# A mixture of experts whose rows go back to their tokens: by scatter to memory, or by matmuls with gate matrices

## The reference

```
logits = h @ w_router + b_router                 # 320 x 32
top_v, top_e = top_k(logits, 4); gate = softmax(top_v)
# for each expert e, for the rows h that chose it:
gu = h @ w_gu[e] + b_gu[e]                       # 1024 -> 2048
gt, up = split(gu); gt = min(gt, 7); up = clip(up, -7, 7)
act = gt * sigmoid(1.702 * gt) * (up + 1)
out = act @ w_dn[e] + b_dn[e]                    # 1024 -> 1024
y[token] += gate * out                           # four experts per token
y = rmsnorm(x + y) * norm_final
```

## Time and profile before

| | |
|---|---|
| median of 3 runs | 1360.87 us (1360.17 to 1361.69) |
| span of the profiled execution (first to last instruction) | 1356.2 us |
| TensorE busy | 1264.1 us, 93% |
| VectorE, ScalarE, POOL busy | 34%, 17%, 9% |
| chain that ended last | TensorE 74%, DMA 23% |
| HBM read, written | 477.57 MB, 22.61 MB |

### The profile page before, as it was taken

How to read it: one execution, slowest core, us unless ns; L and a number is a source line. 1 busy time by engine, 2 the same in 40 slices (tenths; PEclk the granted TensorE clock), 3 DMA queues, 4 the chain that set the end, 5 groups by cost and what they waited for, 6 DMA issues and landing times.

```text
span 1356.2 us, 14399 instructions
## 1 busy us (share of the span) xinstructions
PE 1264.1 (93%) x5895; PEld 570.1 (42%) x5895; DVE 459.0 (34%) x809; ACT 230.7 (17%) x333; POOL 123.2 (9%) x164
## 2 busy tenths in 40 slices
PE   7999999999999999999999999999987778878786
PEld 5756766666543333333333333333322223222231
DVE  2897322211463322223113313222422222233226
ACT  4102432310221111111011111111211111111121
POOL 3110100000010100000000000100010000000020
PEclk9999999999999999999999999999999999999898
DMA  9715826465699999999999999999999999999994
GB/s 331 258 63 157 266 76 156 155 248 204 254 364 426 425 426 426 426 425 427 426 425 427 427 427 424 425 427 425 424 427 425 425 427 425 425 426 426 424 388 153
DMA packets 97115, 479.33 MB, mean 353 GB/s; under 512 B 43962, under 2 KB 46026, under 8 KB 72311
## 3 DMA queue, kind: packets, MB, share of 16 engines
q1 hardware_dynamic: 84641, 459.36, 83.3%
q0 software_dynamic: 11008, 15.63, 3.3%
q10 hardware_dynamic: 1374, 3.02, 0.6%
HBM read 477.57 MB, written 22.61 MB: 369 GB/s over the span
## 4 chain that ended last, share of the span: by engine, by line
PE 74%; DMA 23%; issue 1%; DVE 1%; ACT 0%; DVEq 0%; ACTq 0%
PE PS L1762 29%; PE PS L1400 15%; PE PS L1795 14%; DMA ring<-in_w_dn 12%; DMA ring<-in_w_gu 11%; PE PS L1340 4%; PE PS L1580 4%; PE PS L1624 3%; PE PS L1436 2%; PE PS L1847 1%; PE PS L1667 0%; PE PS L1527 0%; DMA XX<-in_x_prompt 0%; PE PS L1546 0%; PE PS L1644 0%
## 5 line engine op out<-in xcount | busy, mean ns | idle before, releaser
L1762 PE MATMUL PS<-ring,arena 128*64 128x512 f32 x1824 | 405.7, 597 | 39.2 <-DMA ring<-in_w_gu 27.6
L1251 DVE TENSOR_TENSOR arena<-PS,XX 128x1024 f32<-128x1024 f32 x32 | 39.2, 1224 | 659.2 <-PE PS L1762 659.2
L1762 PEld LDWEIGHTS PS<-ring,arena 128*64 128x64 f32 x1824 | 129.2, 139 | 293.7 <-issue 291.1
L1795 PE MATMUL PS<-ring,arena 128*64 128x512 f32 x896 | 203.7, 604 | 16.9 <-DMA ring<-in_w_dn 15.6
L1400 PE MATMUL PS<-arena,ring 128*128 128x320 f32 x768 | 213.5, 434 | 0.1
L1400 PEld LDWEIGHTS PS<-arena,ring 128*128 128x128 f32 x768 | 144.3, 190 | 58.7 <-issue 2.0
L1762 PE MATMUL PS<-arena 128*64 128x512 f32 x608 | 136.3, 595 | 11.6 <-DMA arena<-in_w_gu 10.8
L854 ACT ACTIVATE arena<-arena 128x1024 f32<-128x1024 f32 x32 | 33.9, 1058 | 618.4 <-DVE arena L1254 618.4
L554 POOL DMA_INDIRECT y_rows<-arena x60 | 59.8, 996 | 791.7 <-ACT arena L835 762.9
L1795 PEld LDWEIGHTS PS<-ring,arena 128*64 128x64 f32 x896 | 62.0, 139 | 142.0 <-issue 142.0
L1340 PEld LDWEIGHTS PS<-ident,arena 128*128 128x128 f32 (+3 forms) x580 | 63.1, 142 | 54.8 <-issue 49.0
(11 more groups left out here) (216 smaller groups left out, 670.2 us busy)
## 6 DMA issues: line engine op xcount, KB each, us to landing
ring<-in_w_gu SPq DMA_DIRECT2D x96, 2048.0 KB, 27.9
ring<-in_w_dn SPq DMA_DIRECT2D x48, 2048.0 KB, 29.3
arena<-in_w_gu SPq DMA_DIRECT2D x31, 2048.0 KB, 28.7
arena<-in_w_dn SPq DMA_DIRECT2D x16, 2048.0 KB, 30.0
ring<-in_w_in SPq DMA_DIRECT2D x11, 2048.0 KB, 11.3
ring<-in_w_mem_kv SPq DMA_DIRECT2D x2, 2048.0 KB, 20.7
ring<-in_cache_mem_k SPq DMA_DIRECT2D x32, 128.0 KB, 3.3
ring<-in_cache_mem_v SPq DMA_DIRECT2D x4, 1024.0 KB, 6.1
```

Source lines behind the costliest of these rows:

```text
L1251: nc.vector.tensor_tensor(gbuf[:], PS[:, 0:2, :], g_bias, ALU.add).then_inc(main["g_added"], 1)
L1762: last = mm(PS[64 * h:64 * h + 64, 2 * g + b, :], in_block(xT[:, k, :], b), (spare[kk] if m == BONUS else moe_ring(m, 2)[:, kk]) [:, g * D ...
L1795: last = mm(PS[64 * h:64 * h + 64, 4 + b, :], actT[:, b, j, c * BLK:(c + 1) * BLK], moe_ring(m, 4)[:, j, h * 512:(h + 1) * 512], start=c = ...
```

## The change

Every expert's rows are now added to the tokens on chip. There is no scatter, no zero fill and no reading back of ranks. Instead:

- The positions R (the slot of each token in each expert) and dense gates GD are turned once on TensorE into rows of experts (`turn_places`), four copies on the partitions, and kept by ScalarE in RG. Per expert VectorE spreads the expert's row to all partitions by a shuffle of 2 x 320 columns and makes a matrix W of slots x tokens for each block: one where the token's position is the slot, times the gate (`gate_weights`).
- TensorE multiplies W with Zs of expert e - 2 amid the gate-up of expert e (tiles 0 and 1 after its second piece, tile 2 after its third), into banks that transposes and down products use otherwise; VectorE adds each sum to X at once (`add_tokens`). The last expert's sum is at the very end, after the skip of the code for over 128 rows.
- Fetches: instead of one indirect DMA of 4 KB rows there are four of quarter rows (1 KB). The slots lie so that a VectorE transpose of 32 x 32 blocks gives xT (`turn_tokens` on VectorE); TensorE's token turns and ScalarE's copies go, but for expert 1.
- Blocks are contiguous halves of the 128 slots (before: even and odd). Pieces 2 and 3 of a gate-up, with their second blocks together, are freed at its end; both down pieces at the end of the down part.

The diff, cut to its core:

```diff
-    if c == 3:
+    if c in (2, 3):
         return "gu_done", NE, e + 1
-    if c == 5:
+    if c in (4, 5):
         return "dn_done", NE, e + 1
...
-            sp.wait_ge(main["scattered"], 32 * NE * (w + 1))
+            sp.wait_ge(main["dn_done"], NE * (w + 1))
...
         def gather(v, e):
             if NE * v + e > 1:
-                pool.wait_ge(main["xt_turned"], NE * v + e - 1)
-            nc.gpsimd.indirect_dma_start(
-                out=XG[e % 2][:], out_offset=None, in_=h_rows,
-                in_offset=bass.IndirectOffsetOnAxis(ap=TG[min(v, 1)][:, e:e + 1], axis=0),
-                bounds_check=T - 1, oob_is_err=False).then_inc(main[f"gathered{e % 2}"], 16)
-        def scatter(v, e):
-            pool.wait_ge(main["zs_ready"], NE * v + e + 1)
-            for b in range(2):
-                nc.gpsimd.indirect_dma_start(
-                    out=y_half, out_offset=bass.IndirectOffsetOnAxis(ap=ZI[min(v, 1)][:, b, e:e + 1], axis=0),
...
+                pool.wait_ge(main["xT_ready"], NE * v + e - 1)
+            for s in range(Q):
+                nc.gpsimd.indirect_dma_start(
+                    out=XG[e % 2][:, 256 * s:256 * (s + 1)], out_offset=None, in_=h_quarters,
+                    in_offset=bass.IndirectOffsetOnAxis(ap=TG[min(v, 1)][:, s, e:e + 1], axis=0),
+                    bounds_check=Q * T - 1, oob_is_err=False).then_inc(main[f"gathered{e % 2}"], 16)
...
+        def add_tokens(v, g, tt):
+            i = GROUPS * v + g
+            dve.wait_ge(main["tok_done"], TT * i + tt + 1)
+            if i:
+                dve.wait_ge(main["tok_added"], TT * (i - 1) + tt + 1)
+            add_sums(tt, g == NE - 2).then_inc(main["tok_added"], 1)
+
+        def gate_weights(v, e):
...
+            nc.vector.stream_shuffle(RGs[:], RG, mask=[e] * 32).then_inc(main["rows_spread"], 1)
+            dve.wait_ge(main["rows_spread"], n)
+            for b in range(2):
+                last = nc.vector.scalar_tensor_tensor(W[e % 2][:, b, :], RGs[:, 0, :], slotpos[:, b:b + 1], RGs[:, 1, :],
+                                                      ALU.is_equal, ALU.mult)
+            last.then_inc(main["w_ready"], 1)
+
+        def turn_tokens(v, e):
+            dve.wait_ge(main[f"gathered{e % 2}"], 16 * Q * ((NE // 2) * v + e // 2) + 16 * (e % 2))
+            nc.vector.transpose(xT[:].rearrange("p k (s l) -> p s k l", s=Q), XG[e % 2].rearrange("p (s q k) -> p s k q", s=Q, k=KT)).then_inc(main["xT_ready"], 1)
...
         def window(v):                                   # VectorE
             for e in range(NE):
                 n = NE * v + e + 1
...
+                if e >= 2:
+                    for tt in range(TT):
+                        add_tokens(v, e - 2, tt)
                 dve.wait_ge(main["spread_ready"], n)
                 dve.wait_ge(main["gu_done"], n)
...
                 nc.vector.tensor_tensor(ubuf[:], PS[:, 2:4, :], u_bias, ALU.add).then_inc(main["gu_read"], 1)
+                if e + 1 < NE and n > 1:
+                    turn_tokens(v, e + 1)
...
                     .then_inc(main["act_ready"], 1)
+                if e + 1 < NE:
+                    spread_bias(v, e + 1)
+                if e:
+                    gate_weights(v, e - 1)
...
             for c in range(4):                           # TensorE, gate_up
+                await_chunk(v, AT[(e, c)])
+                if v == 0 and c == 2 and e < 2:
+                    pe.wait_ge(main["xT_ready"], e + 1)
+                if c < 2:
+                    second_block(v, count, lambda: products(c, 1))
+                    products(c, 0).then_inc(main["chunk_used"], 1)
+                elif c == 2:
+                    products(2, 0)
+                else:
+                    second_block(v, count, later_half)
+                    products(3, 0).then_inc(main["gu_done"], 1)
+                between(c)
...
+        def block_sum(e, tt, b, start, stop, last):
+            for h in range(2):
+                ins = mm(token_sum(tt, h, last), W[e % 2][64 * h:64 * h + 64, b, tt * P:tt * P + ROWS[tt]],
+                         Zs[64 * h:64 * h + 64, b, :], start=start, stop=stop)
+            return ins
...
+                def between(c):
+                    if n == 0 and c == 0:
+                        first_list()
+                    if n == 0 and c == 2:
+                        move_list(0)
+                    if e and c == (1 if n == 1 else 0):
+                        turn_act(v, e - 1)
+                    if e >= 2 and c in (1, 2):
+                        tiles = range(2) if c == 1 else (2,)
+                        if c == 1:
+                            pe.wait_ge(main["actT_ready"], n)
+                            pe.wait_ge(main["zs_ready"], n - 1)
+                            pe.wait_ge(main["w_ready"], n - 1)
+                        else:
+                            pe.wait_ge(main["tok_added"], TT * (GROUPS * v + e - 2) + 1)
...
+                        to_tokens(v, e - 2, counts[e - 2], tiles, n > 2, False, main["tok_done"])
...
+            to_tokens(v, NE - 2, counts[NE - 2], range(TT), True, True, None)
+            down(v, NE - 1, counts[NE - 1])
+            pe.wait_ge(main["zs_ready"], NE * (v + 1))
+            pe.wait_ge(main["w_ready"], NE * (v + 1))
...
+        window(0)
         with pe.If(most > WIN):
...
+        last_tokens(0, bd_done)
```

More of the change, by code:

```diff
@@ L31 @@
 RING = 8
-SKIP = 1 << 22
+SKIP = 1 << 20
+Q = 4
 PADA, PADB = CA - 1, CB - 1
@@ new lines, in _, with token_sum @@
+            last = nc.vector.tensor_tensor(POS[0:r, tt], R[0:r, tt, None, :].to_broadcast([r, Q, NE]),
+                                           iota_r[0:r, None, :].to_broadcast([r, Q, NE]), ALU.subtract)
+        last.then_inc(dense_ready, 1)
+        fetch_list(0)
+        def token_sum(tt, half, last):
+            r = ROWS[tt]
+            if last:
+                return PS[:, 2 * tt + half, :] if tt < 2 else PS[64 * half:64 * half + r, 7, :]
+            return PS[:, 6 - 2 * tt + half, :] if tt < 2 else PS[64 * half:64 * half + r, 6, :]
@@ new lines, in gate_up, with products, later_half @@
+        def gate_up(v, e, count, between):
+            n = NE * v + e
+            def products(c, b):
+                m = AT[(e, c)]
+                if n == 0 and c == 0 and b == 1:
+                    pe.wait_ge(main["xT_ready"], 1)
+                turns = [(kk, g) for kk in range(2) for g in range(2)] if c else [(kk, g) for g in range(2) for kk in range(2)]
+                for kk, g in turns:
+                    k = 2 * c + kk
+                    if c == 0 and kk == 0 and n:
+                        pe.wait_ge(main["gu_read" if g else "g_added"], n)
+                    for h in range(2):
+                        last = mm(PS[64 * h:64 * h + 64, 2 * g + b, :], xT[:, k, BLK * b:BLK * (b + 1)],
+                                  (spare[kk] if m == BONUS else moe_ring(m, 2)[:, kk])
+                                  [:, g * D + h * 512:g * D + (h + 1) * 512],
+                                  start=k == 0, stop=k == KT - 1)
+                return last
+            def later_half():
+                products(2, 1)
+                products(3, 1)
+            for c in range(4):
+                await_chunk(v, AT[(e, c)])
[10 more added lines that the diff above has]
+                between(c)
@@ new lines, in token_sum, with bias_sum @@
+        def token_sum(tt, half, last):
+            r = ROWS[tt]
+            if last:
+                return PS[:, 2 * tt + half, :] if tt < 2 else PS[64 * half:64 * half + r, 7, :]
+            return PS[:, 6 - 2 * tt + half, :] if tt < 2 else PS[64 * half:64 * half + r, 6, :]
+        def bias_sum(tt):
+            pe.wait_ge(bdn_in, 32)
+            for half in range(2):
+                rows = slice(NE * half, NE * (half + 1))
+                mm(token_sum(tt, half, False), GT[rows, tt * P:tt * P + ROWS[tt]], bdn[rows, :], start=True, stop=False)
@@ L1842, in to_tokens, with window @@
-        def to_tokens(x, tt):
-            r = ROWS[tt]
-            rows = ubuf if x else Zs
-            for b in range(2):
-                for h in range(2):
-                    last = mm(token_sum(tt, h), W[x][64 * h:64 * h + 64, b, tt * P:tt * P + r], rows[64 * h:64 * h + 64, b, :],
-                              start=False, stop=x == 1 and b == 1)
-            return last
-        def window(v, lo=0, hi=NE):
-            if v:
-                turn_tokens(v, 0)
-            for e in range(lo, hi):
+        def window(v):
+            counts = {}
+            for e in range(NE):
```

554 lines of the change are left out of this document (202 added, 352 removed).

## The result

The changed kernel takes 1406.05 us (median of 4 runs, 1405.27 to 1407.02), the kernel before took 1360.52 us beside it (4 runs). The ratio is 1.034, 95% interval [1.0324, 1.0353]: 3.4% or 45.5 us slower. A second chip gave 1.0354 [1.0337, 1.0371]. The forecast was 1391 us in a range of 1376 to 1408.

What follows compares the result with a forecast made beforehand. TensorE bounds the first part, the expert weight stream the rest. Sums delay expert 17 by 48.2 us, the stream runs dry, and the first final addition comes 30.4 us later: span 1386.6, plus 4.7 gives 1391 us, range 1376 to 1408.

Steps and rivals of the forecast that it cites:

- The mechanism: Unhidden sums delay TensorE until expert 17, the weight stream runs dry, and the lost stream time comes back nowhere.
- the sign: Whole kernel: slower, chance 0.90, against faster 0.08 and same 0.02.
- Sums, unhidden until expert 17: TensorE's queue until expert 17's gate-up ends: 21 blocks of sums at 2.79 us add 58.6 us; removed turns save 16.4.
- Once-only work and the start: TensorE in expert 0 to 2: bias products, turning places and gates add 6 us (4 to 9); stepped first-token loads cost nothing.
- 946 us for expert 17: End of expert 17's gate-up on TensorE: 897.8 us before, 48.2 us later with the change.
- A dry queue, then 5.03 us a piece: After expert 17's gate-up: weight queue empty, first piece lands 7.3 us later, then 81 pieces at 5.03 us (4.94 to 5.12).
- The forecast's 1360.7 us: Landing of the last weight piece: 953.3 us plus 81 pieces of 5.03 us; before the change it was 1330.5 us.
- Release of places: Weight ring: two next pieces are requested together at the gate-up's end, 946 us, the first landing at 953.3 us at the earliest.
- VectorE: Per expert: strided turn takes 1.9 us (1.2 to 2.1), hidden by 1.7 us; additions, some 3.8 us, fill idle time.
- Gathers: Four fetches an expert take some 22 us, issued almost two experts (49 us) ahead of use: hidden.
- Tail: After the last landing: products end 5.6 us later, copy 1.0, jump 6.3 (3 to 9), first tile's sum 0.9; first addition 1374.5 us.

Runs made afterwards that it cites:

- the repeated run: The changed kernel as it is, run once more on the chip of three of the other runs: 1407.5 us (1403.7 to 1409.5).

## Why the prediction was right, and where it was not

The mechanism, the sign and the range held. By its steps:

- **Sums, unhidden until expert 17: right.** From expert 1's gate-up to expert 17's it was 485.2 us before and is 532.5 now, 47.3 us more; sums, turns and bias products had been put at 45.2. The missing 2.1 us fit about 0.15 us at each switch between kinds of products (3.58 us a quarter after a sum, 3.43 without), which is argued from these rows and not tried.
- **Once-only work and the start: wrong, the costliest step.** Up to expert 0 I had set the cost of the stepped loads at "no price", since the turns' loads with the same step take 187 ns. A product's load is another thing: 336 ns. With the clock that fell it made 10.4 us at expert 0; then 4.1 us until expert 1, where 3 had been counted. A part of that is the second fall of the clock (3.4 us at 410.4 us): the repeated run, which lacks it, has 2.9. The rule of the Trainium skill ("SBUF — State Buffer", note on cachelines) had been set aside for the one row that could mislead. Its 3 us were right for the last 24 products, which took 3.1 us more; they lacked the first 24 (2.3 us) and the clock's part (2.4 to 4.4 us).
- **946 us for expert 17** became 959.6: 10.4 + 1.1 + 2.1.
- **A dry queue, then 5.03 us a piece: right.** The second piece requested lands at 959.97 + 12.5 = 972.5 us; 80 more at 5.03 make 1374.9; the last one lands at 1339.8 + 35.6 = 1375.4 us. The forecast's 1360.7 us is missed by the 13.6 us of expert 17 and 1.1 more.
- **Release of places: right, its price not named.** I had the two requests at the gate-up's end at expert 17, and so they came; the sum holds the wait but doesn't say that it is 4 to 5 us of the 45.5. It is no part of the miss.
- **VectorE: right.** The turn takes 2.04 us (1.9 forecast), the additions 1.22 and twice 0.69, and from 491 to 960 us TensorE is busy for 469.00 of 469 us.
- **Gathers: right.** The stream's pace is 5.02 us a piece (5.03 forecast), and 5.00 with whole rows.
- **Tail: short by 3.5 us.** Landing to the last product 6.8 us (5.6 forecast), time without work at the jump 7.4 (6.3), first tile's sums 2.1 (0.9), since the clock fell to 0.50 at 1386.6 us, in the gap, and the sums of the last expert ran at half speed (12 in 5.68 us):

```profile
1390.67 5.68 PE L1776 MATMUL PS<-arena,XX 64*128 64x512 f32 x12 [8.48 <-issue]
...
1392.80 1.23 DVE L1149 TENSOR_TENSOR XX<-PS,XX 128x1024 f32<-128x1024 f32 x1 [21.98 <-PE PS L1776]
```

VectorE's first final addition starts at 1392.8 us, forecast 1374.5: 14.7 + 3.5 us. From it to the end it is 12.1 us, as before.

So the forecast of +30.4 us missed 18.3 of the 48.7 us of span: some 13.6 at the start and first part, 1.1 until the last landing, 3.6 in the tail. The measured 1406.05 us lie 2 us below the upper end of the range, though the loads and the clock were in none of its terms: that the range held is in part luck, as it had been made wide for other causes.

**What stays open.** Why a transpose's load with step 8 takes 199 ns where a product's takes 336. In the same stage, with the same step, from X where the products read XN, at full clock:

```profile
L1273 PEld LDWEIGHTS PS<-ident,XX 64*128 64x128 f32 x8 | 1.0, 199 | 0.0
```

A turn is one such load and a product is two, which is a difference and not yet a reason. Why slow loads bring the clock down, and why the jump was 4.5 us in one run, is open as well.

## What to carry to other kernels

Work moved onto the busiest engine is paid in full as long as that engine has no gap, and costs next to nothing once a stream decides: read the two stretches apart, and put such work into the second. Here a transfer queue that stood nearly empty at its start passed the delay of its first requests on to the end, whatever reserve it had later. Before a layout changes, look for a row with the same operation and the same operand's step, not one that only looks alike; and where the Trainium skill warns and the row is of another kind of operation, keep its case in the range. And before a difference between two profiles is given to an edit, compare them at a point that lies before the edit.

## What the runs showed of the hardware

- A 128-column fp32 load for a product takes 190, 193 to 198, 255 to 264, 329 and 336 ns at steps of 1, 2, 3, 4 and 8 elements, all read at full clock; steps 2 and 3 are from one execution.
- With stepped loads from 366.9 to 370.4 us on the granted clock was at 0.50 within 1 to 6.2 us, for 13.7 to 20.5 us, in each of ten profiles; in five of them it fell again for 3.4 us at 407 to 411 us; TensorE was listed as busy nearly all the while. The mixed steps 2 and 3 had it too. The four kernels with plain loads (the one before among them) had 1.00 there.
- A gap of 8.5 us in the tail lowered the clock too, 4.4 us after the last product, and it stayed low for 10.2 us.
- The taken jump over the code for over 128 rows left TensorE without work for 7.4 us, 4.5 in one run; taken before the gate-up of expert 31 it left a gap of 3.8 us there, and 1.17 us remained between the copy and the sums.
